# Two places more for expert tiles, a seventeenth place for gathered rows, and a new order on block two's way into its gathers

## The chip, the cores and the metric

The kernel runs on one core of one Trainium2 chip. The metric is the time of one execution on the device in microseconds (us). A profiled execution has a span of its own, from its first to its last instruction.

## The reference

Two transformer blocks are computed one after the other over 256 tokens of width 1024, all in float32.

- Block one: modulation vectors from `silu(c) @ w_ada`; a mixer made of a gated convolution, neighbourhood attention and a gated delta rule; then a mixture of experts. There are 32 experts of three matrices each (`w1`, `w3` of 1024x512, `w2` of 512x1024), and each token takes the best two of its group: `(silu(x @ w1) * (x @ w3)) @ w2`. All experts are read whatever the tokens choose, 96 matrices of 2 MiB.
- Block two: gated linear attention (GLA) and block attention (MoBA), an output projection, and PEER: for each token, 8 heads choose 16 of 16384 rows each, by the best 16 of 128 keys in two halves, the best 16 of their 256 sums, and a softmax over these. With the rows u and v of the chosen entries,

```
w[t, h, k] = gate[t, h, k] * gelu(u[idx[t, h, k]] . x[t])
out[t]    += sum over h, k of w[t, h, k] * v[idx[t, h, k]]
```

## The kernel before

**The ring.** `ring` is six slots of 2 MiB (16 KiB on each of 128 partitions). SyncE (SP) issues every load of weights in one order written out by hand; each slot has a semaphore `landed`, and TensorE counts `w_used` up when it has begun on the work behind a tile. SP waits in order: a tile whose slot isn't free holds back all behind it.

**The experts** go in 16 pairs. For each pair p TensorE computes in this order: `first_layer(p, "a")` with tiles 0 and 1 of the pair (`w1` of both experts), `first_layer(p, "b")` with tiles 2 and 3 (`w3`), `gathered(p + 1)` (the next pair's tokens are picked by a matmul), the transposes, `scattered(p - 1)`, and the two `y` products with tiles 4 and 5 (`w2`). L1598 is a matmul of the first layer (64 to a pair, "a" then "b"), L1639 one of `y`, L1553 of `gathered`, L1609 of `scattered`. The tiles are loaded in the order 0 to 5 of pair 0, then 0 to 5 of pair 1, and so on: the slot of tile l of pair p+1 is that of tile l of pair p. `w_used` is raised by 2 at the first matmul of "b" (tiles 0 and 1 free), of `gathered` (2 and 3) and of the next "a" (4 and 5). Behind the experts come block two's twelve tiles: six of `w_in_2`, two of `w_out_2`, four of `peer_w_query`.

**Block two** runs on a list of jobs, `block2_jobs`: each job is a PSUM bank (job number modulo 6) that TensorE fills and DVE ("D") or ACT ("A") empties. Each engine's program is written in its own fixed order, and each waits in order. Names that matter here, for the second half of the tokens (t = 1) or the first (t = 0): `q00` and `q01` are the queries of PEER's head pairs 0 and 1 of t = 0, `sc00` and `sc01` their scores against the keys; `p10` to `p13`, `o1` are the turned attention weights and the attention output of MoBA (L1745); `st2` and `go10`, `go11` the state and outputs of GLA (L1786, L1789); `yT10`, `yT11` the turned mixer output (L1669); `wo10`, `wo11` the output projection (L1195); `xT10`, `xT11` the turned input of the remaining queries. TensorE's order is: `query(0, 0)`, keys, `sc00`, GLA's scores, `p1x`, `st2`, `o1`, `go1x`, then all of `query(0, 1)` and `sc01`, then `yT1x`, `wo10`, `wo11`, `xT1x`.

**Routing.** DVE's `route(r, part, head)` is 25 small parts; part 21 writes the row indices and raises `idx_ready` (L2907). For the first head it stands in DVE's program between the pieces of MoBA and GLA: `moba_out(1)` (L2728 to L2735) stands ahead of parts 11 to 21.

**The gathers.** There are 256, i = 0 to 255 (16 for each head and half of the tokens): `indirect_dma_start` on GpSimd (L1978) brings u and v for 128 tokens, 8 KiB to a partition, 1 MiB in all. `uv_plan` gives each gather a place and what it must wait for: a job of block two after which that memory is free, or `v_free`, TensorE's count of finished values. Sixteen places: 12 in ring slots and four elsewhere in SBUF; the ring slots come free only with the jobs `wo10`, `wo11`, `q10` to `q13`. So for most of the late queries only eight are there: gather i + 8 waits for value i. Then DVE's `dot(i)` (L2921) takes the gathered u times x, ACT applies gelu, DVE multiplies by the gate (`weights`, L2930), ACT writes a diagonal matrix (L1135), and TensorE adds the values, four matmul instructions each (`values`, L1830). The batches of `gelu` and `weights` are of 2 up to value `EARLY` = 64, then of 4.

**The late queries** stand between the values: six queries, each in `STEPS` = 5 steps, four with two values and a quarter of the query (L1678) and one with two values and the scores (L1819). Value 4 is the first of this stretch, value 60 the first behind it.

**The head.** In block one's beginning TensorE projects `k0`, `k1` (L1239), then `gab` (16 gate columns, L1195 with 128x16), then `q0`, `q1`, `v0`, `v1` (L1189); `warm(n)` is n fillers on TensorE (L1209). Further on DVE takes four reciprocals in a row (L2136) that stand behind the job `gc` in its program.

Of the kernel before, what the change touches and what calls it, by code (L numbers as in the profile page):

```python
# [115 lines left out]
def head_jobs():  # L116
# [10 lines left out]
    for name in ("gab", "q0", "q1", "v0", "v1"):  # L127
        add(name, "D")
# [135 lines left out]
STEPS = 5  # L264


def block2_jobs():
# [11 lines left out]
    jobs += some("D", "xT01", "s10", "s11", "s12", "s13") + some("A", "q00", "kst10", "kst11")  # L279
    jobs += some("D", "sc00", "at10", "at11", "p10") + some("A", "p11") + some("D", "p12") + some("A", "p13")  # L280
    jobs += some("D", "st2", "o1") + some("A", "go10", "go11", "q01", "sc01", "yT10")
    jobs += some("D", "yT11", "wo10", "wo11") + some("A", "xT10") + some("D", "xT11")
# [33 lines left out]
UV_PLACES = 16  # L316
EARLY = 64
# [36 lines left out]
def two_blocks(nc, io):  # L354
    ctx = ExitStack()
    with ctx:
# [85 lines left out]
        sil_d = W(7936, 4, T)  # L442
        act_d = W(8960, 4, T)
# [50 lines left out]
        qp = [[W(9216, 4, P), W(8192, 4, P), W(6656, 4, P), W(6656, 4, P)],  # L494
# [69 lines left out]
        landed = [sem(f"landed{i}") for i in range(RING)]  # L564
        w_used = sem("w_used")
# [121 lines left out]
        def slot(i, cols=512):  # L687
# [3 lines left out]
                  mod[:, 0:2, :].rearrange("p a d -> p (a d)")]  # L691
# [17 lines left out]
        def _(sp):  # L709
# [56 lines left out]
            with sp.Fori(1, N_EXP // 2) as i:  # L766
                for l in range(6):
                    sp.wait_ge(w_used, i * 6 + (l - 3))
                    expert_tile(i * 2 + l % 2, l, (N_HEAD + l) % RING)
            for i in range(len(tiles2)):  # L770
                n2 = N_HEAD + N_MOE + i
                if i < RING:
                    sp.wait_ge(w_used, N_MOE + i - 3)
# [11 lines left out]
        def _(act):  # L785
# [60 lines left out]
            conv_silu("k0", 4)  # L846

# [12 lines left out]
            centre_tap("q0", 0)  # L860
# [246 lines left out]
            query(0, 0)  # L1107
# [4 lines left out]
            query(0, 1)  # L1112
            key_scores(0, 1)
# [24 lines left out]
            for h in range(2):  # L1138
                exp_gates(gates[:, 0, h, :], h + 1)
            applied(0, 4)  # L1140
            root(5)
            features_in("xT", 1, cols2)
            at = 4
            for j, (t, g) in enumerate(LATE_QUERIES):
                turn = 2 * (STEPS * j + 4)
# [8 lines left out]
        def _(pe):  # L1154
# [102 lines left out]
            key_chunk(7, 2 * P, 0, 0)  # L1257
# [1807 lines left out]
```

## Time and profile before

| | |
|---|---|
| median of 3 runs | 1620.18 us (1619.58 to 1621.11) |
| the profiled execution, its own time | 1622.18 us |
| its span | 1620.4 us |
| mean granted TensorE clock | 0.965 |
| TensorE busy | 90% of the span |
| DVE, ACT, GpSimd busy | 49%, 18%, 19% |
| bytes read by DMA | 548.39 MB, 339 GB/s over the span |
| the chain that ended last | PE 49%, DMA 38%, issue 5%, DVE 5% |

The busy shares are means over very different stretches. The row of bytes moved in forty slices of 40.5 us, the first below, shows where the time is set by memory and where it is not.

### The profile page before, as it was taken

The page shows a single profiled execution, that of the slowest core. Times are in us where ns is not written, and L with a number is a line of the kernel's source. Part 1 is how long each engine was busy: PE and PEld are TensorE (multiplying, and loading weights), DVE is VectorE, ACT ScalarE, POOL GpSimd, SP SyncE. Part 2 cuts the span into 40 slices and gives each one's busy share as a digit, 9 for nine tenths or more (in the row PEclk, how much of TensorE's full clock was granted, in tenths as well). Part 3 has the DMA queues.
Part 4 walks back from the last instruction along what each step waited for, and adds up shares of the span by engine and source line. Part 5 has one row for each costly group of instructions (what it writes and reads, how often), then busy time and mean ns, then how long its engine had stood idle before and what let it go on. Part 6 is the DMA issues. An engine that isn't in the chain of part 4 may idle for free.

```text
span 1620.4 us, 16884 instructions
## 1 busy us (share of the span) xinstructions
PE 1456.6 (90%) x6246; PEld 789.7 (49%) x6246; DVE 787.2 (49%) x1864; ACT 289.6 (18%) x702; POOL 311.4 (19%) x291
## 2 busy tenths in 40 slices
PE   7999999899999999999999888889788777877778
PEld 5887875544444444444546655555333333333333
DVE  2256645332232322322524558465767576757544
ACT  1422431100000000000243222122122111111111
POOL 0001000100000000000000024353564444444441
PEclk9999999999999999999999989999998999899999
DMA  9642456399999999999625058999999999999997
GB/s 361 272 151 104 157 205 263 107 431 428 426 429 428 427 428 427 425 426 428 282 96 223 7 185 357 394 422 407 392 422 421 421 421 421 422 421 421 421 422 290
DMA packets 60371, 550.58 MB, mean 340 GB/s; under 512 B 8704, under 2 KB 8992, under 8 KB 10368
## 3 DMA queue, kind: packets, MB, share of 16 engines
q1 hardware_dynamic: 22336, 277.47, 41.4%
q0 software_dynamic: 37952, 271.99, 41.0%
q8 instruction: 53, 0.87, 0.2%
q14 instruction: 30, 0.25, 0.0%
HBM read 548.39 MB, written 1.05 MB: 339 GB/s over the span
## 4 chain that ended last, share of the span: by engine, by line
PE 49%; DMA 38%; issue 5%; DVE 5%; ACT 2%; POOL 1%; SPq 0%; DVEq 0%; POOLq 0%; ACTq 0%
DMA ring<-expert_w_d 17%; DMA ring<-peer_uv_d,work 14%; PE ps L1830 10%; PE ps L1598 8%; PE ps L1195 7%; DMA mod<-peer_uv_d,work 5%; PE ps L1678 4%; PE ps L1189 4%; PE ps L1314 3%; PE ps L1473 2%; PE ps L1203 1%; PE ps L1639 1%; PE ps L1553 1%; PE ps L1320 1%; POOL ring L1978 1%
## 5 line engine op out<-in xcount | busy, mean ns | idle before, releaser
L1830 PE MATMUL ps<-ring,work 128*128 128x512 f32 x728 | 354.4, 630 | 76.4 <-ACT work L1135 76.3
L2921 DVE CUSTOM_DVE_ANT_0 ring<-ring,work 128x1024 f32<-128x1024 f32 x182 | 222.2, 1222 | 120.0 <-DMA ring<-peer_uv_d,work 118.3
L1830 PEld LDWEIGHTS ps<-ring,work 128*128 128x128 f32 x728 | 141.9, 200 | 267.4 <-issue 165.9
L1978 POOL DMA_INDIRECT ring<-peer_uv_d,work x182 | 199.1, 1094 | 245.7 <-PE ps L1830 166.1
L1598 PE MATMUL ps<-ring,work 128*64 128x512 f32 x1024 | 225.6, 593 | 10.0 <-DMA ring<-expert_w_d 9.1
L1598 PEld LDWEIGHTS ps<-ring,work 128*64 128x64 f32 x1024 | 78.4, 137 | 154.0 <-issue 153.0
L1135 ACT ACTIVATE work<-consts_sb,work 128x128 f32<-128x128 f32 x256 | 85.1, 392 | 251.0 <-DVE work L2930 239.4
L1195 PE MATMUL ps<-ring,hT 128*128 128x512 f32 (+1 forms) x288 | 119.3, 571 | 1.7 <-ACT hT L996 0.8
L1830 PE MATMUL ps<-work 128*128 128x512 f32 x148 | 83.5, 693 | 35.5 <-ACT work L1135 35.5
L1639 PE MATMUL ps<-ring,work 128*64 128x512 f32 x512 | 113.4, 595 | 0.7 <-DVE work L2486 0.7
L2482 DVE TENSOR_TENSOR work<-work,ps 128x512 f32<-128x512 f32 x16 | 11.0, 687 | 198.7 <-PE ps L1598 198.7
L1954 POOL DMA_DIRECT2D mod<-subkeys_d x1 | 0.6, 555 | 487.5 <-DVEq L2541 487.5
L976 ACT ACTIVATE work<-ps 128x512 f32<-128x512 f32 x16 | 9.6, 597 | 445.4 <-PE ps L1598 445.4
L1195 PEld LDWEIGHTS ps<-ring,hT 128*128 128x128 f32 x288 | 53.9, 190 | 59.9 <-issue 56.6
L1678 PEld LDWEIGHTS ps<-hT,ring 128*128 128x128 f32 x640 | 76.9, 195 | 11.5 <-issue 11.5
L1678 PE MATMUL ps<-hT,ring 128*128 128x128 f32 x640 | 77.8, 279 | 0.0
L1639 PEld LDWEIGHTS ps<-ring,work 128*64 128x64 f32 x512 | 35.3, 137 | 67.4 <-issue 66.5
L1830 PEld LDWEIGHTS ps<-work 128*128 128x128 f32 x148 | 29.9, 215 | 74.3 <-ACT work L1135 45.2
L1553 PEld LDWEIGHTS ps<-work 128*128 128x128 f32 x512 | 60.0, 196 | 12.2 <-issue 12.2
L2493 DVE TENSOR_TENSOR work<-ps,mod 128x512 f32<-128x512 f32 x32 | 22.1, 691 | 89.2 <-PE ps L1639 89.2
L1189 PE MATMUL ps<-hT,ring 128*128 128x256 f32 x288 | 64.7, 386 | 0.0
L1553 PE MATMUL ps<-work 128*128 128x128 f32 x512 | 62.9, 283 | 0.0
(417 smaller groups left out, 1652.2 us busy)
## 6 DMA issues: line engine op xcount, KB each, us to landing
ring<-expert_w_d SPq DMA_DIRECT2D x96, 2048.0 KB, 15.7
ring<-w_ada_d SPq DMA_DIRECT2D x12, 2048.0 KB, 7.9
ring<-w_in_d SPq DMA_DIRECT2D x12, 2048.0 KB, 17.5
ring<-w_out_d SPq DMA_DIRECT2D x4, 2048.0 KB, 7.7
ring<-peer_w_query_d SPq DMA_DIRECT2D x4, 2048.0 KB, 8.3
ring<-peer_uv_d,work POOLq DMA_INDIRECT x182, 23.3
ring<-w_in_d SPq DMA_DIRECT2D x2, 1024.0 KB, 22.9
mod<-b_ada_d SPq DMA_DIRECT2D x1, 2048.0 KB, 23.2
```

The source lines that it names most:

```text
L1135: act.activation(diag[:, k % 4, :], ident, ACT.Copy, scale=w_cur[:, s, k:k + 1]).then_inc(diag_ready, 1)
L1189: last = pe.matmul(b[0:n, at:at + T], wt[:, k, c0:c0 + n], hT[:, k, :], start=(k == 0), stop=(k == KC - 1))
L1195: last = pe.matmul(b[:, at:at + n], hT[:, k, t * P:(t + 1) * P], wt[:, k, c0:c0 + n], start=(k == 0), stop=(k == KC - 1))
L1314: last = pe.matmul(b[:, h * P:(h + 1) * P], lhsT(h), rhs(h), start=True, stop=True)
L1473: last = pe.matmul(ps[MID.bank(f"w{t}{n}")][:, :], mixT[k][:, t * P:(t + 1) * P], slot(N_HEAD - 2 + n)[:, k, :], start=(k == 0), stop=(k = ...
L1553: last = pe.matmul(b[:, c * P:(c + 1) * P], h_tok[:, t, k * P:(k + 1) * P], pm[:, t, :], start=(t == 0), stop=(t == TT - 1))
L1598: last = pe.matmul(b[u * CAP:(u + 1) * CAP, :], xeT[:, k, u * CAP:(u + 1) * CAP], wt[u][:, k, :], start=(k == 0), stop=(k == KC - 1), skip ...
L1639: last = pe.matmul(b[u * CAP:(u + 1) * CAP, :], actT[:, c, u * CAP:(u + 1) * CAP], wt[u][:, c, n * 512:(n + 1) * 512], start=(c == 0), sto ...
L1678: last = pe.matmul(b[0:n, at:at + P], wt[:, k, c0:c0 + n], hT[:, k, t * P:(t + 1) * P], start=(k == 0), stop=(k == KC - 1))
L1830: last = pe.matmul(ps[V_BANK[t] + n][:, :], diag[:, i % 4, :], v_row(i)[:, n * 512:(n + 1) * 512], start=(i % (16 * PH) == 0), stop=(i % ( ...
L1978: pool.indirect_dma_start(out=uv_rows(i), out_offset=None, in_=io["peer_uv"], in_offset=bass.IndirectOffsetOnAxis(ap=idx[:, s, k:k + 1], a ...
L2921: dve.tensor_tensor_reduce(out=u_row(i), in0=u_row(i), in1=h_tok[:, i // (16 * PH), :], scale=1.0, scalar=0.0, op0=ALU.mult, op1=ALU.add, ...
```

## The change

Four things, in one diff.

1. **Expert tiles.** Two places more, `beside[0]` and `beside[1]`, each of two pieces of 1 MiB in SBUF that is free while the experts run. Tiles 0 and 1 of every odd pair go there, in two DMAs each; tiles 0 and 1 of the even pairs stay in ring slots 0 and 1, and are asked for ahead of tiles 2 to 5 of the odd pair before them. The first two `beside` tiles are asked for right behind tile 5 of pair 0. Slots 0 and 1 take block two's first two tiles after pair 14. The path for over 64 tokens to an expert, which these inputs don't take, is rewritten to match.
2. **Block two.** `q00` is emptied by DVE; routing parts up to 21 of the first head go ahead of `moba_out(1)`; `query(0, 1)` is cut in two, one half ahead of `yT1x` and one behind `wo11`, and `sc01` moves behind value 5; fillers stand in four places (4, 6, 6 and 4 of them). The late queries begin with value 6 and end with value 65; `EARLY` is 72.
3. **Gathers.** A seventeenth place, in memory that is free once `o1` is done; it takes gathers 1 and 7 and no more, since later scores are written there.
4. **The head.** `q0` is first, its matmuls alternate with those of `gab`; `modulation(3)` stands one piece earlier; `warm(10)` becomes `warm(5)`.

```diff
@@ the head, jobs and TensorE
-    for name in ("gab", "q0", "q1", "v0", "v1"):
+    for name in ("q0", "gab", "q1", "v0", "v1"):
...
+            modulation(3)
             key_chunk(7, 3 * P, T, 0)
-            modulation(3)
             columns(1)
-            warm(10)
+            warm(5)
...
+            for c in range(2):
+                for k in range(KC):
+                    last = pe.matmul(b[:, c * T:(c + 1) * T], wt[:, k, c * P:(c + 1) * P], hT[:, k, :],
+                                     start=(k == 0), stop=(k == KC - 1))
+                    side = pe.matmul(gates[:, 16 * c:16 * c + 16], hT[:, k, c * P:(c + 1) * P], tail_w[:, k, 0:16],
+                                     start=(k == 0), stop=(k == KC - 1))
@@ the plan of the gathers
-    done = {q: 2 * (STEPS * j + 4) for j, q in enumerate(LATE_QUERIES)}
-    steps = [("q00", (13,)), ("go11", (12,)), ("yT10", (14,)), ("wo10", (0, 1)), 2, ("wo11", (2, 3)), ("row", (15,))]
+    done = {q: FIRST + 2 * (STEPS * j + 4) for j, q in enumerate(LATE_QUERIES)}
+    steps = [("q00", (13,)), ("o1", (16,)), ("go11", (12,)), ("yT10", (14,)), ("wo10", (0, 1)), 2, ("wo11", (2, 3)), 4,
+             ("row", (15,)), FIRST]
...
-            for i in range(v, min(step, n - UV_PLACES)):
-                plan.append((plan[i][0], None, i + 1))
+            for i in range(v, step):
+                if len(plan) < n and (plan[i][0] != 16 or i < 2):
+                    plan.append((plan[i][0], None, i + 1))
...
-UV_PLACES = 16
-EARLY = 64
+UV_PLACES = 17
+EARLY = 72
@@ SyncE, the expert tiles
-            with sp.Fori(1, N_EXP // 2) as i:
-                for l in range(6):
-                    sp.wait_ge(w_used, i * 6 + (l - 3))
-                    expert_tile(i * 2 + l % 2, l, (N_HEAD + l) % RING)
+            def beside_tile(e, u):
+                for c in range(2):
+                    sp.dma_start(beside[u][c], io["expert_w1"][e, :, c * 2048:(c + 1) * 2048]
+                                 .rearrange("p (a b) -> p a b", a=4)).then_inc(beside_landed[u], 16)
+
+            for u in range(2):
+                beside_tile(2 + u, u)
+            with sp.Fori(0, PAIRS // 2 - 1) as i:
+                for l in range(2):
+                    sp.wait_ge(w_used, i * 12 + (l + 3))
+                    expert_tile(i * 4 + (4 + l), l, (N_HEAD + l) % RING)
+                for l in range(2, 6):
+                    sp.wait_ge(w_used, i * 12 + (l + 3))
+                    expert_tile(i * 4 + (2 + l % 2), l, (N_HEAD + l) % RING)
+                for u in range(2):
+                    sp.wait_ge(w_used, i * 12 + (u + 9))
+                    beside_tile(i * 4 + (6 + u), u)
+                for l in range(2, 6):
+                    sp.wait_ge(w_used, i * 12 + (l + 9))
+                    expert_tile(i * 4 + (4 + l % 2), l, (N_HEAD + l) % RING)
+            for l in range(2, 6):
+                sp.wait_ge(w_used, 6 * (PAIRS - 2) + l + 3)
+                expert_tile(N_EXP - 2 + l % 2, l, (N_HEAD + l) % RING)
@@ TensorE, block two
             query(0, 0)
             gla_keys(1)
+            warm(4, V_BANK[0] + 1)
             key_scores(0, 0)
             gla_scores(1)
+            warm(6, V_BANK[0] + 1)
             moba_turned(1)
             gla_state(2)
+            warm(6, V_BANK[0] + 1)
             moba_values(1)
             gla_values(1)
-            query(0, 1)
-            key_scores(0, 1)
+            query_part(0, 1, 0)
+            query_part(0, 1, 1)
             pe.wait_ge(tok_ready, 3)
             to_features("yT", 1, y2)
+            warm(4, V_BANK[0] + 1)
             out_projected(1, 0)
             values(0, 2)
             out_projected(1, 1)
             values(2, 4)
+            query_part(0, 1, 2)
+            query_part(0, 1, 3)
+            values(4, FIRST)
+            key_scores(0, 1)
             pe.wait_ge(tok_ready, 4)
             to_features("xT", 1, x)
-            at = 4
+            at = FIRST
@@ DVE, block two
+            btook(dve.tensor_copy(qp[0][0], b4(bjob("q00"))))
...
-            routes(0, 5, 11, 0)
+            routes(0, 5, 8, 0)
             gla_state(2)
+            routes(0, 8, 22, 0)
             moba_out(1)
-            routes(0, 11, 22, 0)
+            routes(0, 0, 3, 1)
             gla_out(1)
-            routes(0, 0, 5, 1)
+            routes(0, 3, 5, 1)
             features_in("yT", 1, 1)
-            routes(0, 22, PARTS, 0)
-            routes(0, 5, 12, 1)
...
+            dot(0)
+            routes(0, 22, PARTS, 0)
+            dot(1)
+            routes(0, 5, 7, 1)
+            weights(0)
+            dot(2)
+            out_added(1, 0)
+            dot(3)
+            routes(0, 7, 10, 1)
+            weights(1)
+            dot(4)
+            routes(0, 10, 22, 1)
+            dot(5)
+            out_added(1, 1)
+            squares(1, 5)
+            weights(2)
+            dot(6)
+            row_normed()
+            dot(7)
+            routes(0, 22, PARTS, 1)
```

## Rows read from the trace of the kernel before

**Rows 1.** The page: GB/s moved in 40 slices of the span
```profile
GB/s 361 272 151 104 157 205 263 107 431 428 426 429 428 427 428 427 425 426 428 282 96 223 7 185 357 394 422 407 392 422 421 421 421 421 422 421 421 421 422 290
```
**Rows 2.** Stretches: time, busy us (count) of each engine, clock, DMA share, GB/s
```profile
600.00:700.00 100.00, 97.90 (x480) 42.42 (x478) 28.39 (x67) 2.39 (x4) 0.00 (x0) 1.00 1.01 426
930.00:985.00 55.00, 48.98 (x210) 31.73 (x209) 32.70 (x105) 15.75 (x38) 13.44 (x12) 0.90 0.52 188
985.00:1170.00 185.00, 158.66 (x635) 93.09 (x634) 115.46 (x335) 40.40 (x112) 82.58 (x72) 0.96 1.00 407
1170.00:1600.00 430.00, 345.50 (x709) 142.67 (x708) 279.38 (x693) 80.37 (x238) 191.75 (x173) 0.92 1.01 421
```
**Rows 3.** The chain of waits in the experts: start, us, what
```profile
338.23 13.73 PE ps L1598 x64
...
366.83 6.87 PE ps L1598 x32
...
727.63 7.09 PE ps L1598 x32
...
735.60 21.96 DMA ring<-expert_w_d
...
757.70 7.10 PE ps L1598 x32
```
**Rows 4.** SyncE's queue in order of time, around the experts' begin
```profile
280.32 0.33 SPq L755 DMA_DIRECT2D ring<-expert_w_d  x1
...
320.16 0.97 SPq L755 DMA_DIRECT2D ring<-expert_w_d  x2
```
**Rows 5.** The head: instructions of PE and DVE, and a stretch
```profile
37.47 2.48 PE L1209 MATMUL ps<-consts_sb 128*128 128x128 f32 x20
46.69 3.75 PE L1195 MATMUL ps<-tail_w,hT 128*128 128x16 f32 x32
50.30:53.80 3.50, 3.50 (x10) 2.85 (x11) 0.37 (x2) 2.74 (x6) 0.57 (x1) 0.54 1.00 422
```
**Rows 6.** Block two before the gathers: stretches, and TensorE in order of time
```profile
923.90:937.20 13.30, 13.30 (x53) 11.50 (x53) 6.73 (x22) 3.38 (x12) 1.97 (x2) 0.50 0.15 50
...
904.62 7.41 PE L1678 MATMUL ps<-hT,ring 128*128 128x128 f32 x64
...
934.14 9.02 PE L1678 MATMUL ps<-hT,ring 128*128 128x128 f32 x64
...
944.86 1.04 PE L1669 MATMUL ps<-consts_sb,work 128*128 128x128 f32 x8
946.73 7.11 PE L1195 MATMUL ps<-ring,hT 128*128 128x512 f32 x16 [0.83 <-ACT hT L990]
```
**Rows 7.** DVE in order of time: first scores, MoBA's output, row indices
```profile
915.89 0.75 DVE L2828 TENSOR_SCALAR work<-ps,small 128x512 f32<-128x512 f32 x1 [4.13 <-PE ps L1819]
...
926.95 0.69 DVE L2731 TENSOR_TENSOR work<-ps,small 128x512 f32<-128x512 f32 x1 [1.50 <-PE ps L1745]
...
932.35 0.17 DVE L2905 CAST work<-work 128x16 uint32<-128x16 f32 x1
```
**Rows 8.** GpSimd in order of time: gathers 0, 3, 9 and 16
```profile
933.51 1.01 POOL L1978 DMA_INDIRECT consts_sb<-peer_uv_d,work  x1 [46.37 <-DVEq L2907]
...
954.64 0.94 POOL L1978 DMA_INDIRECT ring<-peer_uv_d,work  x1 [7.44 <-PE ps L1195]
...
980.33 1.41 POOL L1978 DMA_INDIRECT mod<-peer_uv_d,work  x1 [7.79 <-DVEq L1999]
...
994.80 1.56 POOL L1978 DMA_INDIRECT ring<-peer_uv_d,work  x1 [3.40 <-issue]
```
**Rows 9.** TensorE in order of time: values 10 and 60
```profile
999.09 1.98 PE L1830 MATMUL ps<-work 128*128 128x512 f32 x4 [1.63 <-ACT work L1135]
...
1146.31 1.98 PE L1830 MATMUL ps<-ring,work 128*128 128x512 f32 x4 [1.63 <-ACT work L1135]
```

**Rows 10.** L1978 from 930 to 985: a gather's time from issue to landing
```profile
DMA to landing us min/median/max: 5.3/6.4/7.5
```

More of the change, by code:

```diff
@@ L564, in two_blocks @@
         landed = [sem(f"landed{i}") for i in range(RING)]
+        beside_landed = [sem(f"beside_landed{u}") for u in range(2)]
         w_used = sem("w_used")
@@ L1136, in applied @@
                                        scale=w_cur[:, s, k:k + 1]).then_inc(diag_ready, 1)
-            for h in range(2):
-                exp_gates(gates[:, 0, h, :], h + 1)
+            exp_gates(gates[:, 0, 0, :], 1)
             applied(0, 4)
+            exp_gates(gates[:, 0, 1, :], 2)
+            applied(4, FIRST)
             root(5)
+            query(0, 1)
+            key_scores(0, 1)
             features_in("xT", 1, cols2)
-            at = 4
+            at = FIRST
             for j, (t, g) in enumerate(LATE_QUERIES):
-                turn = 2 * (STEPS * j + 4)
+                turn = FIRST + 2 * (STEPS * j + 4)
                 applied(at, turn)
@@ L1538, in fbank, with expert_tile @@
                 return ps[FAST.bank(name)]
-            def expert_tile(p, l, cols=512):
-                m = 6 * p + l
-                pe.wait_ge(landed[(N_HEAD + m) % RING], 16 * (m // RING + 1))
-                return slot(N_HEAD + m, cols)
+            def expert_tile(p, l):
+                if l < 2 and p % 2:
+                    pe.wait_ge(beside_landed[l], 32 * (p // 2 + 1))
+                    return lambda k: beside[l][k // 4][:, k % 4, :]
+                pe.wait_ge(landed[(N_HEAD + l) % RING], 16 * ((p // 2 if l < 2 else p) + 1))
+                wt = slot(N_HEAD + l, 512 if l < 4 else 1024)
+                return lambda k: wt[:, k, :]
             def gathered(p):
@@ L1562, in _ @@
             with pe.If(many == 1):
-                with pe.Fori(0, N_EXP // 2) as i:
-                    for u in range(2):
+                with pe.Fori(0, PAIRS // 2) as i:
+                    for q, u in ((0, 0), (0, 1), (1, 0), (1, 1)):
+                        job = 16 * q + 8 * u
                         for r in range(2):
-                            wi = N_HEAD + 2 * r + u
-                            pe.wait_ge(landed[wi % RING], i * 16 + 16 * ((wi - N_HEAD) // RING + 1))
-                            wt = slot(wi)
+                            wt = slot(N_HEAD + 2 * r + u)
+                            column = lambda k, c: wt[:, k, c:c + P]
+                            if r == 0 and q:
+                                pe.wait_ge(beside_landed[u], i * 32 + 32)
+                                column = lambda k, c: beside[u][k // 4][:, k % 4, c:c + P]
+                            elif r == 0:
+                                pe.wait_ge(landed[(N_HEAD + u) % RING], i * 16 + 16)
+                            else:
+                                pe.wait_ge(landed[(N_HEAD + 2 + u) % RING], i * 32 + 16 * (q + 1))
@@ L1635, in _ @@
                         b = fbank(f"y{p}{n}")
-                        wt = [expert_tile(p, 4 + u, 1024) for u in range(2)]
+                        wt = [expert_tile(p, 4 + u) for u in range(2)]
                         for c in range(4):
@@ L1659, in b2_tile @@
             def b2_tile(i):
-                m = N_MOE + i
-                pe.wait_ge(landed[(N_HEAD + m) % RING], 16 * (m // RING + 1))
-                return slot(N_HEAD + m)
+                experts = PAIRS // 2 if i % RING < 2 else PAIRS
+                pe.wait_ge(landed[(N_HEAD + i) % RING], 16 * (experts + i // RING + 1))
+                return slot(N_HEAD + i)
             def to_features(name, t, src):
@@ L2986, in _ @@
                     assert bt[0] == len(b_mine)
[L2987 to L2994 removed]
+                if 10 <= i < 23:
+                    routes(1, 2 * (i - 10), min(2 * (i - 10) + 2, PARTS))
                 elif i >= 32:
```

122 lines of the change are left out of this document (57 added, 65 removed).

## The prediction

> **What bounds the kernel now.** I read the page first, for the row of bytes in forty slices [rows 1]: two plateaus at 421 to 431 GB/s, the experts (320 to 795 us) and the gathers (from about 985 us on), and between them, around 800 to 985, a valley down to 7 GB/s. Then stretches [rows 2] for what each plateau moves and what the valley lacks; the chain of waits in the experts [rows 3]; SyncE's queue where they begin [rows 4]; the engines in order of time in the head and in the valley [rows 5 to 9]; and how long a gather takes to land [rows 10]. The reader is to see this: from 1170 on memory is never idle, so the end can only move by as much as the bytes of the gathers begin earlier, or by work saved ahead of them.
>
> A gather is 1.0486 MB, 2.49 us at 421 GB/s [rows 2]; 256 take 637.6. From 930 to 985 memory moved 188 GB/s for 55 us [rows 2], 10.3 MB, which is 24.6 us at the full rate: the gathers stand as if they had run at full rate from 960.4. Between 985 and 1170 they ran at 407 [rows 2]: 185 us times 14/421, 6.2 us more lost. 960.4 + 637.6 + 6.2 = 1604.2, and the last values, the result and the output take the rest of the span. I call 960.4 the gathers' virtual begin.
>
> **Experts: the two places.** SP asked for tile 5 of pair 0 at 280.32 and got its next free slot at 320.16 [rows 4]; tile 5 has landed by 298, and memory then has nothing to do until 320. Two beside tiles (2.1 MB each, 4.92 us at 426 GB/s) fit into that hole, so the stream of experts ends 9.8 us earlier. Does TensorE? A pair that waits for nothing takes 338.23 to 366.83, 28.6 us [rows 3]; a pair of six tiles takes memory 29.5. What TensorE waits for is "b" of each pair: from 735.60 a DMA of 21.96 us, and "b" of pair 15 begins at 757.70 [rows 3]. So the tile that counts is tile 3 of a pair. I count tiles asked for from 320.16 on. Before, the order is 0 to 5 of pair 1, then of pair 2: tile 3 of pair p is number 6(p-1)+4. After, it is 0 and 1 of pair 2, then 2 to 5 of pair 1, 0 and 1 of pair 3, 2 to 5 of pair 2: tile 3 of pair p is again number 6(p-1)+4, up to pair 14. The tiles that come earlier are 0 and 1, for which nobody waited. Only pair 15 has nothing ahead of it: its tile 3 is number 86 in place of 88, 9.8 us earlier. But "b" of pair 14 still begins at 727.63, and 28.6 later is 756.2: TensorE gains 757.7 - 756.2 = 1.5 us. Against it, 14 of the tiles move as 8 KiB rows in place of 16; the gathers, 8 KiB rows too, reach 421 where whole tiles reach 426 [rows 2], 14 x 4.92 x 1.2% = 0.8 at most. I take 1 us gained; bounds 1 us lost and 9.8 gained. Block two's first tiles come from the same queue two tiles earlier; before, TensorE didn't wait for them.
>
> The Trainium skill (DMA: Bandwidth & Descriptors, Anatomy of one DMA) gives each DMA about 2 us of fixed cost beside its bytes, for those that GpSimd issues. By that, halving 14 tiles would add 14 x 2 = 28 us, an estimate, if it were paid one after the other. The trace speaks against it: gathers of 1 MiB follow each other at 421 GB/s [rows 2].
>
> **The head.** `gab` alone is 3.75 us of very short matmuls, and right behind it the granted clock is 0.54 for 3.5 us [rows 5]: 1.2 GHz in place of 2.4, 1.6 us lost. Between the matmuls of `q0` the same 32 keep their cost (each needs a weight load about as long as the 0.117 us that it takes now), but TensorE has no thin stretch, and I expect the clock to stay: 1.6. Five fillers fewer are 1.24 us [rows 5], of which only the part beyond the wait for hT is gained: 0.4. Everything to 305 us hangs on this chain, through `gc` and DVE's four reciprocals. `modulation(3)` one piece earlier only shifts a copy that was waited for by nobody: nothing. `q0` ahead of `gab` delays the gates by 7 us; they are needed at 97, with some 35 us in hand. Sum 2; bounds 0 (the clock falls somewhere else) and 5.5 (the gate matmuls disappear, 3.7).
>
> **Block two, on the old clock.** First the order without gathers. `q00` is done at 912.0 (904.62 + 7.41 [rows 6]); ACT is busy with MoBA's exps, so the scores reach DVE at 915.89 [rows 7]. With DVE copying (0.7), four fillers (0.25 each [rows 5]) and 1.1 us of scores, DVE reads them at 914.4: 1.5 saved. `moba_out` and its wait (1.50 and a product of 0.69 at 926.95 [rows 7], a second like it, a reciprocal and the syncs) leaves the way to the indices: 3.2. So the indices are there at 927.9 in place of 932.6 [rows 7], gather 0 at 928.9, gather 1 at 930.1 in the new place (`o1` is done by 924.5), gather 2 at 931.4.
>
> The clock is 0.50 from 923.9 to 937.2 [rows 6], behind a stretch in which TensorE waited for DVE. The 10.2 us up to the end of `go11`, 934.14 [rows 6], would be 5.1 at 2.4 GHz. If the fillers hold the clock, 4.7 of that are gained: `go11` at 929.4. Half of `query(0, 1)`, 3.6, ends at 933.0; DVE has the row of y at 933.9; `yT10` is done at 934.5 in place of 945.4 (944.86 and half of the 1.04 [rows 6]), because TensorE no longer does the whole query, 9.02 from 934.14 on [rows 6], and its scores first. Gather 3 goes at 935.4. `wo10` (7.1 [rows 6]) ends at 943.1, gathers 4 and 5 go at 944 and 945; before, 3 and 4 went at 954.64 [rows 8]. Values 0 and 1 follow at once (their dots are done by 939): places free at 945 and 946.6, gathers 6 and 7. `wo11` ends at 953.6: 8, 9; values 2 and 3: 10, 11 at 956 and 958. DVE: dot 4 at 949.5, the second head's indices at 955, dot 6, and the row for place 15 at 962.8: gather 12 (before, 980.33 for gather 9 [rows 8]). Values 4, 5: 13 and 14 at 965 and 966. Then ACT's turn (root, features, gelu) lets value 6 begin at 969.8 and value 10 at 980.2. Before, value 10 began at 999.09 [rows 9].
>
> From there eight places turn at TensorE's pace of two values and a quarter query, 5.2 us: gather 16 at 977.5 (before 994.80 [rows 8]), 24 at 1001.3. Serving each for 2.49 us, 1.7 after its issue, memory idles 4.7 us ahead of gather 4, then 1.0, 2.7, 0.3 and 3.1, and has done 24 gathers at 1003.0: virtual begin 1003.0 - 24 x 2.49 = 943.2, 17.2 earlier. After that the places (8, then 10, 12, 14 as the late queries end) are just enough, as before: value 10 to 60 took 147.2 us [rows 9], 2.94 for each against 2.49 for a gather, and two new places per ten values make up for it. I count 4 us lost there, against 6.2: there is one value pair more per new place early on, and small batches to value 72 soften the stop behind the late queries. 943.2 + 637.6 + 4 = 1584.8; gain 19.4, I take 19. Bounds: 10 (below) and 24. The price in engines: 20 fillers, 5 us in TensorE's own waits; DVE's copy, 0.7, in its wait for scores; ACT has one move fewer. GpSimd's queue waits in order: a late `o1` would hold gathers 2 to 4, but `o1` precedes `go11` anyway.
>
> **Sum.** The profiled execution took 1622.18 of its own time, 1.8 beside the span of 1620.4, and 2.0 above the median. 1622.2 - 2 - 1 - 19 = 1600.2; against the median, 1598.
>
> **Rivals.** (A) The experts gain the whole 9.8: if the wait at "b" is one for slots and not for the order of bytes, tiles issued a pair ahead help each pair. For it: the chain's DMA pieces begin at a slot's release (735.60). Against: memory moves 426 without a hole. Then 1589. (B) The way into the gathers gains only half: the clock falls all the same, or DVE, ACT and TensorE, which now meet more often, each wait for a gather that lands late (dots stand ahead of the second indices). With `go11` back at 934 and value 6 four or five us later, the virtual begin is 952 and with nothing in the head the sum is 10 to 12: 1609. The clock part has the skill behind it (TensorE: Matmul & The Clock Gate, Part 1): the slow rate is the default, activity releases it, and the point of change varies from run to run; the trace agrees on the fall at 923.9. (C) Late queries set the pace: with eight places and two values more ahead, the lead is spent waiting for places, losses grow from 4 to 20: 1616. Against: value 10 is 19 us ahead of the old one, and at 2.94 a value, value 66 then begins at 1146, where the old value 60 began. (D) Slower: the 28 halves of beside tiles are served one after the other. It needs 0.8 us more for each (22/28) to undo all; with few others in flight a gather of that size takes at least 5.3 to land [rows 10] against 2.49, so up to 28 x 2.8 = 78 us: 1625 to 1675.
>
> **Chances.** Main case 1592 to 1605: 0.60. A (1584 to 1592): 0.10. B (1605 to 1613): 0.20. C: 0.06. D: 0.04. To hold 8 in 10 the range takes the main case, most of B and part of A: 1589 to 1611. A measurement of this kernel tells a change from none at 0.2%, 3.2 us: faster 0.95 (D and a little of C fall out), same 0.02, slower 0.03.
>
> **What would show it.** The clock at 1.00 from 50 to 54 and through the 920s; bytes between 281 and 298 in place of the hole; "b" of pair 14 at the old time less the head's gain, that of pair 15 28.6 later; indices 4.7 earlier against the end of the experts, `yT10` 11 earlier, value 16 15 earlier; 421 GB/s from there. I am wrong if "b" of middle pairs begins earlier, if the clock falls in the 920s, if DVE waits for gathers 4 to 8, or if memory moves under 400 between 1000 and 1100.

## The result and the profile after

The changed kernel takes 1607.3 us (median of 9 runs, 1604.14 to 1614.05), the kernel before, timed on the same chip, 1621.95. The ratio is 0.9904, 95% interval 0.9888 to 0.9921: 15.6 us faster, 12.8 to 18.2. I had forecast 1598, 22 us faster, with a range of 1589 to 1611. The direction and the range held, and so did the steps of the mechanism but one; the gain is 0.7 of what I said. The time lies outside the band that I gave the main case (1592 to 1605) and in that of rival B, whose mechanism the rows below rule out. The profiled execution took 1606.09 of its own, 16.1 under the 1622.18 of the one before.

The page's row of GB/s in forty slices, and stretches of the changed kernel (the columns are those of the rows before: time, busy us and count of PE, PEld, DVE, ACT and POOL, granted clock, DMA share, GB/s):

```profile
GB/s 364 275 154 105 158 204 263 199 419 429 425 427 426 425 426 427 426 426 345 346 38 221 69 284 344 389 420 408 403 405 422 421 421 422 421 422 421 422 421 283
```

```profile
50.30:53.80 3.50, 3.50 (x22) 3.21 (x23) 0.24 (x1) 0.92 (x2) 0.00 (x0) 1.00 0.98 414
302.00:320.00 18.00, 14.95 (x80) 9.10 (x82) 2.92 (x10) 0.60 (x1) 0.00 (x0) 0.91 0.03 10
320.00:340.00 20.00, 19.27 (x108) 9.05 (x106) 5.92 (x15) 0.00 (x0) 0.00 (x0) 1.00 0.97 403
...
600.00:700.00 100.00, 97.25 (x478) 42.12 (x476) 28.24 (x66) 2.39 (x4) 0.00 (x0) 1.00 1.01 426
920.00:940.00 20.00, 18.59 (x115) 14.23 (x114) 17.13 (x57) 7.66 (x19) 3.85 (x4) 1.00 0.52 200
925.00:985.00 60.00, 54.84 (x241) 33.78 (x241) 47.93 (x150) 20.89 (x49) 23.29 (x20) 1.00 0.83 318
985.00:1170.00 185.00, 156.20 (x634) 91.90 (x633) 113.68 (x320) 41.99 (x115) 80.77 (x70) 0.98 0.99 399
1170.00:1200.00 30.00, 30.00 (x71) 13.28 (x70) 22.08 (x55) 8.89 (x23) 20.04 (x18) 1.00 1.00 405
1200.00:1584.00 384.00, 302.08 (x616) 123.69 (x616) 245.84 (x611) 68.16 (x207) 163.58 (x149) 0.92 1.01 421
```

The eighth slice holds 199 GB/s where it held 107 [rows 1]: the two tiles beside the ring fill the hole. These bytes are missing again at the end of the experts, in slices 19 and 20, 345 and 346 for 428 and 282: the stream of experts ends two tiles earlier and finds no free slot. The valley is shorter (284 and 344 where 185 and 357 stood). Behind it come 389, 420, 408, 403 and 405, where 394, 422, 407, 392 and 422 stood: with more bytes moved ahead of it, this stretch still doesn't reach the plateau of 421, and to that I had not given enough weight.

The same arithmetic as in the prediction, on the new rows. From 925 to 985 memory moved 318 GB/s for 60 us, which is 45.3 us at 421: the gathers stand as if begun at 939.7, where they stood at 960.4. That is 20.7 us. From 985 to 1170 they run at 399: 185 x 22/421 = 9.7 us lost, where 6.2 were lost before. From 1170 to 1200 1.1 more are lost at 405, before it was 0.6. 20.7 - 3.5 - 0.5 = 16.7; the profiled executions differ by 16.1.

Most of the growth sits at the front of that stretch. From 985 to 1043 memory moves 376 GB/s, 6.2 us lost, where it moved 404 and lost 2.3; from 1043 to 1170 it moves 409, where it moved 408. The share of time in which the DMA engines are busy falls by 2% against the plateau (0.99 for 1.01) and the bytes by 5% (399 for 421), so part of the loss is idle time and part is engines that are shown busy and move less. Why they move less no run shows.

GpSimd in order of time, gathers 0, 3, 4 and 16:

```profile
927.86 1.02 POOL L2029 DMA_INDIRECT consts_sb<-peer_uv_d,work  x1 [41.55 <-PE ps L1832]
...
933.87 0.94 POOL L2029 DMA_INDIRECT work<-peer_uv_d,work  x1 [2.48 <-PE ps L1712]
942.24 1.90 POOL L2029 DMA_INDIRECT ring<-peer_uv_d,work  x1 [7.43 <-PE ps L1222]
...
975.92 1.71 POOL L2029 DMA_INDIRECT ring<-peer_uv_d,work  x1 [4.27 <-issue]
```

The experts: "b" of pair 14 and of pair 15 on TensorE in order of time, and the sum of TensorE's waits for expert tiles from 320 to 780 (us, times, longest):

```profile
728.25 7.09 PE L1641 MATMUL ps<-ring,work 128*64 128x512 f32 x32 [0.69 <-DMA ring<-expert_w_d]
...
756.91 7.04 PE L1641 MATMUL ps<-ring,work 128*64 128x512 f32 x32
```

```profile
PE ps L1641 <- DMA ring<-expert_w_d: 9.2, 12, 1.7
```

"b" of pair 14 begins 0.6 later than before, that of pair 15 28.66 behind it and waits for nothing. TensorE in order of time among the late queries, lines with a wait, and at the stop behind them:

```profile
1021.03 3.67 PE L1873 MATMUL ps<-ring,work 128*128 128x512 f32 x8 [1.57 <-ACT work L1159]
1027.22 3.70 PE L1873 MATMUL ps<-work 128*128 128x512 f32 x8 [1.63 <-ACT work L1159]
...
1145.42 1.98 PE L1873 MATMUL ps<-ring,work 128*128 128x512 f32 x4 [1.63 <-ACT work L1159]
1149.60 7.50 PE L1873 MATMUL ps<-ring,work 128*128 128x512 f32 x16 [0.47 <-ACT work L1159]
1162.07 3.78 PE L1873 MATMUL ps<-ring,work 128*128 128x512 f32 x4 [4.96 <-ACT work L1159]
```

Value 66 begins at 1145.42; I had said 1146. At each of the six turns of a late query (the place where ACT empties the query's bank, and then that of its scores) TensorE waits twice for ACT, 1.57 to 3.05 us each time, 23.3 us in all. In the kernel before these twelve waits were 20.7.

### The profile page after: what moved, and what is told of

Same layout as the page of the kernel before. It is cut to its first block and busy times, and to the rows that moved or that the text cites. A ratio compares the mean times of both kernels' runs of the same rounds, so it can differ in the third digit from the quotient of the medians.

```text
span 1604.3 us, 17004 instructions
## 1 busy us (share of the span) xinstructions
PE 1443.8 (90%) x6276; PEld 782.1 (49%) x6276; DVE 789.3 (49%) x1867; ACT 292.4 (18%) x705; POOL 311.4 (19%) x291
## 5 line engine op out<-in xcount | busy, mean ns | idle before, releaser
L1873 PE MATMUL ps<-ring,work 128*128 128x512 f32 x720 | 340.3, 622 | 66.4 <-ACT work L1159 66.3
L1641 PE MATMUL ps<-ring,work 128*64 128x512 f32 x768 | 169.4, 593 | 10.0 <-DMA ring<-expert_w_d 9.2
L1641 PEld LDWEIGHTS ps<-ring,work 128*64 128x64 f32 x768 | 59.6, 137 | 117.6 <-issue 116.6
L1682 PE MATMUL ps<-ring,work 128*64 128x512 f32 x512 | 113.4, 595 | 0.7 <-DVE work L2537 0.7
L1721 PEld LDWEIGHTS ps<-hT,ring 128*128 128x128 f32 x640 | 75.7, 192 | 12.8 <-issue 12.7
L1682 PEld LDWEIGHTS ps<-ring,work 128*64 128x64 f32 x512 | 35.3, 137 | 67.4 <-issue 66.5
L2973 DVE CUSTOM_DVE_ANT_0 work<-work 128x1024 f32<-128x1024 f32 x40 | 48.9, 1222 | 28.8 <-DMA work<-peer_uv_d,work 28.4
## 6 DMA issues: line engine op xcount, KB each, us to landing
work<-expert_w_d SPq DMA_DIRECT2D x24, 1024.0 KB, 12.8
```

The source lines that it names most:

```text
L1641: last = pe.matmul(b[u * CAP:(u + 1) * CAP, :], xeT[:, k, u * CAP:(u + 1) * CAP], wt[u](k), start=(k == 0), stop=(k == KC - 1), skip_group ...
L1682: last = pe.matmul(b[u * CAP:(u + 1) * CAP, :], actT[:, c, u * CAP:(u + 1) * CAP], wt[u](c)[:, n * 512:(n + 1) * 512], start=(c == 0), sto ...
L1721: last = pe.matmul(b[0:n, at:at + P], wt[:, k, c0:c0 + n], hT[:, k, t * P:(t + 1) * P], start=(k == 0), stop=(k == KC - 1))
L1873: last = pe.matmul(ps[V_BANK[t] + n][:, :], diag[:, i % 4, :], v_row(i)[:, n * 512:(n + 1) * 512], start=(i % (16 * PH) == 0), stop=(i % ( ...
L2973: dve.tensor_tensor_reduce(out=u_row(i), in0=u_row(i), in1=h_tok[:, i // (16 * PH), :], scale=1.0, scalar=0.0, op0=ALU.mult, op1=ALU.add, ...
```

## The experiments

All ratios are to the kernel before, timed on the same chip, with their 95% interval; 0.001 is 1.6 us. The changed kernel has 0.9904 [0.9888, 0.9921]. A difference between two of these kernels is the difference of their ratios; the two intervals together leave it uncertain by 4 to 5 us.

**e1, e2, e3: the three parts.** The diff falls into the head, the experts and block 2's way, which share no line.

```
e1: before + block 2's way (FIRST, job order, uv_plan, qp, fillers, EARLY, DVE's order)
e2: e1 + the head (q0 with gab between its matmuls, five fillers fewer)
e3: before + the experts (beside tiles, order of asking, acc_s, sil_d, act_d)
```

> The kernel before with only block 2's way changed (job order, fillers, seventeenth place, batches of 2 to value 72); head and experts as before. By my prediction this part is worth 19 us (bounds 10 to 24). By my reading of the changed kernel's trace it starts the gathers' stream 19.9 us earlier and then loses about 4 us more than before while TensorE alternates values and late queries, so it is worth 15 to 16. If the part that I put in the experts (a small loss) were in truth a gain of several us, this kernel would be worth only 8 to 12.

> The changed kernel with the expert stage of the kernel before (six places, no tiles beside the ring). Against the kernel of e1 it shows the head alone: my prediction says 2 us better (TensorE's clock kept from 50 to 54). Against the changed kernel it shows the two places alone: my prediction says that the changed kernel is 1 us better, the rival of the full lead says 9.8 better, and my reading of the trace (1.2 us lost at the branch into the experts) says 0 to 1.5 worse. So the time should be 16 to 18 us under the kernel before, about the changed kernel's own or 1 us under it; the rival wants it 10 us above the changed kernel.

> The kernel before with only the two places more for expert tiles. My prediction: 1 us faster, since tile 3 of a pair keeps its place in the order of asking, so that what TensorE waits for lands when it did. The rival of the full lead: 9.8 us faster. My reading of the changed kernel's trace: between 1 us faster and 1.5 us slower, with the second half of pair 14 beginning 1 us later than in the kernel before, and that of pair 15 28.7 after it in place of 30.1.

Measured: e1 0.9906 [0.9887, 0.9925], 15.3 us; e2 0.9899 [0.9879, 0.9920], 16.4 us; e3 0.9995 [0.9985, 1.0006], 0.8 us. So nearly all of the gain is block 2's way. The head is worth 1.1 us by e2 against e1, give or take 4.5: neither 0 nor 2 can be told from it. The experts are worth 0.8 alone, give or take 1.7, and minus 0.8 on top of e2, give or take 4.3: nothing that can be told from zero. The full lead of 9.8 us is out. The head's clock did what was said; the stretch of e1 and that of e2:

```profile
50.30:53.80 3.50, 3.50 (x11) 2.87 (x11) 0.37 (x2) 2.73 (x6) 0.57 (x1) 0.52 1.01 426
```

```profile
50.30:53.80 3.50, 3.50 (x24) 3.22 (x23) 0.00 (x0) 0.03 (x1) 0.00 (x0) 1.00 0.98 416
```

**e4: the fillers.**

```
-            warm(4, V_BANK[0] + 1)     (two such lines)
-            warm(6, V_BANK[0] + 1)     (two such lines)
```

> The changed kernel without the 20 filler multiplications in block 2's way to the gathers. My prediction says that they hold the clock at 2.4 GHz through the 920s and that this is worth 4.7 us of the first indices: without them the granted clock falls to 0.5 there as it did before, gather 0 comes 4 to 5 us later against the end of the experts, and if the whole stream shifts with it the kernel is 4 to 5 us slower. Rival: the stream is bound later by the places that the gathers have and by TensorE's pace, so that gather 0 comes 4 us later and the end moves by less than 2 us.

Measured: 0.9957 [0.9941, 0.9973], so 8.6 us slower than the changed kernel, give or take 3.7. Both theories had the size wrong, and both had the wrong place. Stretches of e4, and two lines of TensorE in order of time, `gla_state(2)` and the half of `query(0, 1)`:

```profile
920.00:925.00 5.00, 5.00 (x25) 5.00 (x25) 4.51 (x17) 0.00 (x0) 0.00 (x0) 0.50 0.01 3
925.00:930.00 5.00, 5.00 (x18) 3.88 (x18) 3.97 (x16) 0.90 (x5) 1.97 (x2) 0.50 0.29 80
930.00:935.00 5.00, 5.00 (x21) 4.33 (x21) 0.00 (x0) 2.33 (x7) 0.94 (x1) 0.50 0.83 338
935.00:940.00 5.00, 4.96 (x31) 4.72 (x29) 2.67 (x10) 0.58 (x2) 0.00 (x0) 0.67 0.63 211
```

```profile
918.23 7.06 PE L1788 MATMUL ps<-work 128*128 128x64 f32 x32 [2.80 <-DVE work L2827]
...
932.53 6.56 PE L1721 MATMUL ps<-hT,ring 128*128 128x128 f32 x32
```

The granted clock is at the lower of its two levels from 920 to 935, behind a wait of 2.80 us for DVE, where the changed kernel has 1.00. Gather 0 goes at 926.72, 1.1 *earlier* than in the changed kernel (0.9 of that was there already at the end of the experts): DVE, not TensorE, leads to the first indices. What comes late is TensorE's chain: `gla_state(2)` takes 7.06 for 3.76, half a query 6.56 for 3.84, GLA's output doubles; gather 2 is 3.0 late, gather 4 6.5, gather 16 8.3 (984.27 for 975.92), and gather 254 12 in the profiled executions, which differ by 11.1.

**e11: the fillers alone.** The kernel before with the same four lines at the same places.

```
             gla_keys(1)
+            warm(4, V_BANK[0] + 1)
             key_scores(0, 0)
...
```

> The kernel before with nothing but the 20 filler multiplications at the same four places of block 2. Taking them out of the changed kernel cost 8 to 9 us (e4). If the clock alone is the cause, they bring the kernel before 5 to 9 us, over half of the whole change, and the new order of jobs and the place the rest. Rival: the fillers only pay with the new order, since in the old one values wait for the query's scores, the output's turn and its evacuations: under 3 us.

Measured: 0.9971 [0.9952, 0.9990], 4.7 us faster, between the two. The clock is 1.00 from 925 to 940. With e1 and e4: fillers alone 4.7, order and place without fillers about 7 (e4, which holds the head and the experts too), the way with both 15.3. So the two together bring 3.6 us more than their sum, but the intervals leave that uncertain by 5 us, and it isn't shown that they need each other. The reason to think so: without the clock the new order is walked at half pace, and in the old order the whole query and its scores stand in front of `yT10` at either pace.

**e8: sixteen places.**

```
-UV_PLACES = 17
+UV_PLACES = 16
-    steps = [("q00", (13,)), ("o1", (16,)), ("go11", (12,)), ...
+    steps = [("q00", (13,)), ("go11", (12,)), ...
```

> The changed kernel without the seventeenth place (it takes gathers 1 and that of its second turn; the others move up by one or two in the plan). My prediction counts it as part of the start: gather 1 then waits for the same end of GLA's output as its neighbour, values 0 to 5 are little touched, and the stream starts 2 to 4 us later. Theory now (TensorE's pace and the places left behind it decide): 0 to 3 us slower than the changed kernel. A rival in which the place carries much of the gain: 5 us or more slower.

Measured: 0.9917 [0.9893, 0.9941], 2.1 us slower than the changed kernel, an interval that holds zero too. Gather 16 goes 2.4 later (978.37) and the loss from 985 to 1170 is as in the changed kernel, 401 GB/s. By the trace the seventeenth place carries little; by the times alone 5 us is not excluded.

**e10: the small batches.**

```
-EARLY = 72
+EARLY = 64
```

> The changed kernel with batches of two values up to value 64 in place of 72, as in the kernel before. My prediction says that the small batches up to 72 soften the stop behind the late queries, by some 2 us of memory's time. If so this kernel is 1 to 3 us slower than the changed one. Rival: the stop is DVE's work on dots and routing parts, which the batches do not change: the same within 1 us.

Measured: 0.9881 [0.9855, 0.9906]: 3.7 us faster by the point estimate, give or take 4.9, so not slower by the 2 or 3 us that I had allowed for. My claim that small batches to value 72 soften the stop has nothing for it. TensorE in e10 behind the last late query, all lines with a wait from 1140 to 1185:

```profile
1141.94 1.96 PE L1873 MATMUL ps<-mod,work 128*128 128x512 f32 x4 [1.58 <-ACT work L1159]
1179.50 8.83 PE L1873 MATMUL ps<-ring,work 128*128 128x512 f32 x16 [2.09 <-ACT work L1159]
```

There is no stop of 4.96 at all; from 1150 to 1170 memory moves 427 and 420 GB/s where the changed kernel has 422 and 400. In this kernel, then, it is the edit from 64 to 72 that makes the stop: the waits of 0.47 and 4.96 stand, to 0.01 us, in all seven traces with 72 and ACT's turns as they were (the changed kernel, e1, e2, e4, e6, e7, e8). 64 is no cure by itself, for the kernel before has 64 and a stop of 5.71 at 1159.14. What the two have in common is that their batches of two reach beyond the last late query (value 59 there, 65 here), and in e10 they end ahead of it. That each pair of values then costs a turn from ACT to DVE and back, where DVE is busy 9.8 us of 10, is argued, not shown by a run of its own; and e10 lacks the loss only from 1150 on, since from 985 to 1170 it too moves 399 GB/s.

**e5: ACT's turns later.** On the changed kernel:

```
                 turn = FIRST + 2 * (STEPS * j + 4)
-                applied(at, turn)
+                applied(at, turn + 2)
                 query(t, g)
-                applied(turn, turn + 2)
+                applied(turn + 2, turn + 4)
                 key_scores(t, g)
-                at = turn + 2
+                at = turn + 4
```

> The changed kernel with ACT's order at each late query changed: ACT first makes the scaled diagonals of the two values that TensorE does behind the query's last part, and evacuates the query then (the same with the next two values and the query's scores). In the changed kernel TensorE waits 1.6 and 1.6 us at each of the six turns, about 19 us in all between 985 and 1145, and a value takes 2.94 us there against memory's 2.49. Theory now (the loss of the late stretch is TensorE's pace): a value takes 2.6 to 2.7, value 66 begins 15 to 19 us earlier, memory moves over 410 GB/s in place of 399 from 985 to 1170, and the kernel is 4 to 8 us faster than the changed one. My prediction's view (4 us lost there in any case, by the stop of DVE and ACT behind the queries): at most 1 to 2 us faster.

Measured: 0.9847 [0.9822, 0.9873], 9.3 us faster than the changed kernel, give or take 4.9, a little over the upper end. A stretch of e5, and TensorE around one turn:

```profile
985.00:1170.00 185.00, 170.35 (x670) 97.91 (x669) 127.83 (x341) 46.93 (x128) 90.22 (x80) 0.96 1.01 419
```

```profile
1013.47 3.60 PE L1873 MATMUL ps<-ring,work 128*128 128x512 f32 x8
1016.90 1.05 PE L1862 MATMUL ps<-mod,work 128*128 128x128 f32 x8
1017.79 3.60 PE L1873 MATMUL ps<-work 128*128 128x512 f32 x8
```

No wait is left at the turns. Value 66 begins at 1118.62, 26.8 us earlier than in the changed kernel, where 15 to 19 were expected: from turn to turn a value takes 2.52 us, as much as a gather. Memory runs at 419 in place of 399: 185 x 20/421 = 8.8 us. A stop follows behind the queries, of 8.74 us at 1139.33, and memory runs at 422 through it (1123 to 1170). So TensorE's pace between the late queries was what held memory back, since a gather needs a place and a place comes free with a value.

**e12: the same edit on the kernel before.**

> The kernel before with ACT's later turns of e5, and nothing of the change. If TensorE's pace between the late queries is what kept the change at 15 us where its gathers start 20.7 us earlier by memory's clock, the kernel before must gain less from the later turns than the changed one did (9): its memory lost 6.2 us there against 9.7, so 4 to 6 us, and the change is worth 19 to 21 on top of it, near what I predicted. Rival: the later turns are worth the same 9 us in both, and the change's value does not depend on the pace.

Measured: 0.9975 [0.9961, 0.9989], 4.1 us, against 9.3 on the changed kernel. The difference, 5.2, has an uncertainty of 5.5. The change on top of the later turns is worth 0.9847/0.9975 = 0.9872, 20.8 us (the intervals of the two together leave 16 to 26): near the 22 that I had forecast, and by the point estimate above the 15.6 that it brings without them. From 985 to 1170 memory moves 413 GB/s in e12 where it moved 407, 2.6 us, and from 1170 to 1200 421 for 413, 0.6.

**e6: the eight places in turn.**

```
+            with sp.Fori(0, PAIRS // 4 - 1) as i:
+                for m in range(8, 32):
+                    sp.wait_ge(w_used, i * 24 + (m - 5))
+                    expert_tile(i * 8 + (2 * (m // 6) + m % 2), m % 6, m % 8)
...
```

> The changed kernel with the same eight places for expert tiles, but each tile goes to the place that comes free next (tile number modulo eight), so that the tiles are asked for in the order in which TensorE needs them; the slow path for uneven routings is written out for four pairs to fit. My prediction's step says that the two places brought only 1 us because tile 3 of each pair kept its place in the order of asking. If so, here the 9.8 us of memory work done in the hole at 281 to 302 reach it: TensorE's waits for expert tiles, 9.2 us in the changed kernel, go, and the end comes 7 to 9 us earlier than in the changed kernel. Rival: TensorE or the small transfers set the pace anyway and the gain is under 2 us.

Measured: 0.9852 [0.9825, 0.9878], 8.4 us faster than the changed kernel, give or take 5. TensorE's waits for expert tiles from 320 to 780 (the second line is for a tile beside the ring), and SyncE's first tiles:

```profile
PE ps L1643 <- DMA ring<-expert_w_d: 3.4, 3, 2.1
PE ps L1643 <- DMA work<-expert_w_d: 0.7, 1, 0.7
```

```profile
318.53 20.00 SPq L764 DMA_DIRECT2D ring<-expert_w_d  x6
344.32 1.25 SPq L768 DMA_DIRECT2D work<-expert_w_d  x2
```

The waits sum to 4.1 us where 9.2 stood. From the first "a" (310.39) to the second layer of pair 15 (760.89) are 450.5 us, where the changed kernel needs 457.6 (311.41 to 769.04): 7.1 us, for the same bytes, the same eight places and the same hole filled. What differs is the order of asking and, with it, which tile goes to which place; more tiles than before go beside the ring, in two DMAs each (24 of 96 for 16).

**e7: another order with the ring as it is.**

The loop's calls, in words:

```
             with sp.Fori(0, PAIRS // 2 - 1) as i:
-                (tiles 0 and 1 of pair 2i+2, then 2 to 5 of pair 2i+1)
-                (the beside tiles of pair 2i+3, then 2 to 5 of pair 2i+2)
+                (tiles 2 to 5 of pair 2i+1, then 0 and 1 of pair 2i+2)
+                (tiles 2 to 5 of pair 2i+2, then the beside tiles of pair 2i+3)
```

> The changed kernel with only the order of asking changed on SP: the two tiles that have double places are asked for behind tiles 2 to 5 of the pair before theirs, not ahead of them. The order is now that of need, but at the start of pair 1 nothing can be asked for until 326, where the changed kernel asks for two tiles at 319.5. By my step (position in the order times 4.9 us a tile): 9.8 less 6.5 to 7, so tile 3 of a pair lands about 3 us earlier and the kernel is about 3 us faster than the changed one. Rival: no difference within 1 us.

Measured: 0.9931 [0.9907, 0.9955], 4.4 us *slower* than the changed kernel, give or take 4.7. A miss: 3 us faster were expected. SyncE's queue and a stretch of e7:

```profile
326.96 41.95 SPq L762 DMA_DIRECT2D ring<-expert_w_d  x10
```

```profile
320.00:340.00 20.00, 19.27 (x108) 9.06 (x106) 5.07 (x11) 0.12 (x1) 0.00 (x0) 1.00 0.53 210
```

SyncE waits in order, so with tile 2 of pair 1 first nothing is asked for until 326.96, and memory moves 210 GB/s from 320 to 340 where it moved 403: 20 x 193/421 = 9.2 us of work lost, against 9.8 for the two tiles of order. I had put the loss at 6.5 to 7. So "b" of pair 14 begins 416.9 behind the first "a", in the changed kernel 416.8, and "b" of pair 15 waits again (29.5 behind it in place of 28.7). That is 1 us; the other 3 of the 4.4 I can't place, and a single profile doesn't help: it has the clock at 0.94 from 925 to 985.

**e9: both.** The edits of e5 and e6 together.

> The changes of e5 (ACT's turns later) and e6 (expert tiles in the places in turn) together. If they are independent, as memory's clock says (e6 starts the gathers' stream 8 us earlier, e5 keeps memory at 420 GB/s through the late queries), the gains of 9 and 8 us add to 15 to 18 us under the changed kernel, some 1590 us. Rival: the second part of e6's start is lost again, since with memory busy from the first gather on it is TensorE and DVE behind the late queries that have to catch up: 10 to 13 us.

Measured: 0.9789 [0.9763, 0.9816], a median of 1591.99 against 1623.27: 34 us under the kernel before and 18.7 under the changed one. The gains of e5 and e6, 9.3 and 8.4, add. Stretches of e9:

```profile
985.00:1170.00 185.00, 169.01 (x661) 96.67 (x660) 124.67 (x327) 46.15 (x125) 93.11 (x80) 0.97 1.01 418
1170.00:1570.00 400.00, 313.36 (x639) 128.38 (x638) 255.27 (x638) 71.08 (x215) 169.96 (x155) 0.92 1.01 421
```

## Why the prediction was right in kind and 6 us off in size

- **The experts, 1 us (measured 0.8 alone, nothing on top of e2).** Right as far as can be told, and for the reason given: the wait at "b" is set by tile 3's number in the order of asking. The row of pair 15, 28.66 behind pair 14 with no wait, is the forecast one; e6 is the proof from the other side, since the same two places asked for in the order of need do bring 7 to 8 us. Only "b" of pair 14 isn't where I had it: from the first "a" it is 416.84 away, before 415.59, so that 1.25 of the 1.41 us that pair 15 gains are lost ahead of it. Rival A took the right bytes and the wrong order. Rival D is out: the beside tiles move at 403 to 427 GB/s.
- **The head, 2 us (measured 1.1, give or take 4.5).** The clock stays at 1.00 from 50.3 to 53.8, and DVE's last copy into hT comes 2.3 us earlier (286.50 for 288.76). But "a" of pair 0 begins only 0.6 earlier (311.41 for 312.04), since TensorE takes longer at its branch into the experts (below). Where the clock falls from 281 to 298 in both traces, e3 without the new head and e2 with it, "a" begins 3.3 earlier with it (312.52 for 315.78).
- **The way to the gathers.** The indices: 4.7 forecast, 4.85 measured (gather 0 5.65 earlier, less the 0.8 of head and experts), by DVE's order alone as the step had it. The fillers: I gave them 4.7; taking them away costs 8.6, because the slow clock also runs over the half query and into `yT10`, which the step counted at the fast rate only. Gather 16 goes 18.9 earlier, 17 were forecast. The virtual begin comes out at 939.7, where 943.2 less the 3 us of head and experts is 940.2. That the two agree is in part luck: head and experts brought 0.8 of the 3 in these traces, and the way 19.9 where I had 17.2. Rival B is out. One of my signs of being wrong did show: DVE waits 4.19 us for a gather at 949.11, among gathers 4 to 8. The sum had dot 4 at 949.5, so the sign was badly chosen, not the sum.
- **The step that failed is the term of the late stretch: "I count 4 us lost there, against 6.2".** 9.7 are lost, and 1.1 more up to 1200 where 0.6 were. I had TensorE's pace nearly right (2.94 a value forecast, 2.98 from value 10 at 978.46 to value 66 at 1145.42; 980.2 and 56 x 2.94 make 1144.8, by the way, not the 1146 that I wrote) and did not ask what it does to a stream that is ahead: with places fixed, memory can be no further than the places ahead of the last value done. Neither reason that I gave for a smaller loss helped: the small batches make the stop behind the queries (e10), and with one value pair more early on, the front of the stretch loses 6.2 us where it lost 2.3. That is rival C's mechanism at a third of its price: I had let the loss grow from 4 to 20 (16 us, which makes 1614 and not 1616), and it grew by 5.7.
- **What shows that term.** e5 takes the waits out of TensorE's pace and gets 9.3 back, clear of noise and in the trace; on the kernel before, the same edit gets 4.1 (e12). With it the change is worth 20.8, close to what the sum gave for a late stretch without growth in its loss. By the traces the sum misses so: the late stretch was to bring 2.2 and costs 3.5, and 0.5 behind it, 6.2 in all; head and experts bring 2.2 less than the 3 forecast; the way brings 2.7 more.
- **What stays open.** That the loss grows with an earlier begin alone isn't shown. e4 and e7 begin later than the changed kernel (280 GB/s from 925 to 985 for its 318) and then lose more, 385 and 389 GB/s from 985 to 1170 for 399. The kernels in block 2's old order lose less (407 before, 413 in e11). What the new order itself does to this stretch, beside the earlier begin, no run takes apart.

## What to carry to other kernels

More places for a stream help only if the tile that is waited for moves up in the order of asking; write the order down as numbers before and after, and if the late tile keeps its number, let the places rotate. Where a stream is limited by memory later and by an engine's pace now, an earlier start can be worth less than the time by which it is earlier (15.6 us for 20.7 here): look at who frees a place and take the waits out of that engine too. In this kernel the evacuations of the second job (the queries) belonged behind the work that the first job's consumer (TensorE's values) needs next, not in front of it: that was 9.3 us.

## What was not expected of the hardware

- TensorE's idle time at the branch into the experts, put down to "issue", differs between kernels: 2.31 us in the kernel before, 3.47 in the changed one, and 3.65 in e12, whose code differs from the kernel before only in ACT's order in block 2. Over all traces it goes from 2.25 (e1) to 4.68 (e10). The four fillers behind it (eight instructions in the trace) take 1.16 in the first and 2.02 to 2.08 in the other two; that is the granted clock, 1.00 from 305 to 306 in the kernel before and 0.50 in the changed one. It is not lost: from there to "a" of pair 0 both take 7.15 us, since in the kernel before the clock falls a microsecond later. TensorE in e12 and in the changed kernel:

```profile
308.90 2.08 PE L1209 MATMUL ps<-consts_sb 128*128 128x128 f32 x8 [3.65 <-issue]
```

```profile
304.26 2.02 PE L1236 MATMUL ps<-consts_sb 128*128 128x128 f32 x8 [3.47 <-issue]
```

  I had thought of the beside tiles, in flight just then; e2 has none and shows 3.11. What sets the idle time stays open.
- With the same head, the profiled executions reach "a" of pair 0 between 312.04 (before) and 315.78 (e3), with a granted clock from 281 to 298 of 1.00 in the first and 0.71 in the second. A single profile of one part of the change can be off by more than the part is worth; for the parts only the timed ratios decide.
- The clock dips between 960 and 1000 in some traces and not in others: from 960 to 980 it is 1.00 in the changed kernel, e2 and e10, 0.91 in e1, e4 and e8, 0.87 in e6 and 0.83 in e7 and e9. An early start of the gathers is not what they share, for e7 starts 3.6 us later than the changed kernel. In e6, which starts 8.1 ahead, gather 24 is only 4.0 ahead behind that stretch. From 985 to 1170 memory moves 385 to 393 GB/s in e1, e4, e6 and e7 and 398 to 401 in the changed kernel, e2, e8 and e10. What makes the clock fall in one and not in the other stays open.
